# Latent attention of a hybrid diffusion backbone: outputs by token, negated maxima, three score banks, and a head's preparation spread over iterations

## What is computed

```python
def diff_attend(q1, q2, k1, k2, v, lam):
    p1 = softmax(einsum(q1, k1) * DIFF_HD ** -0.5)
    p2 = softmax(einsum(q2, k2) * DIFF_HD ** -0.5)
    return einsum(p1 - lam * p2, v)

def mla_attend(qn, qr, kn, kr, v):                 # 8 heads
    s = einsum(qn, kn) + einsum(qr, kr)            # 64 + 32 wide
    p = softmax(s * (64 + 32) ** -0.5)
    return einsum(p, v)                            # v: 64 wide
```

## Time and profile before

| | us |
|---|---|
| median of three runs | 2402.88 (2399.14 to 2410.18) |
| profiled execution | 2399.36 |
| span of its records | 2397.2 |
| TensorE busy | 2262.1 (94%) |
| VectorE, ScalarE busy | 1054.6 (44%), 855.0 (36%) |
| latent attention, layer 0 | 643.6 to 768.4 |
| latent attention, layer 1 | 1963.8 to 2040.3 |

### The profile page before, as it was taken

One profiled execution on the slowest core, in us unless ns is written; L12 is line 12 of the kernel. 1 busy time (PEld: TensorE's weight loads), 2 busy tenths in 40 slices (PEclk: granted clock), 3 DMA queues, 4 the chain that ended last, 5 costly groups with the idle time before them and its releaser, 6 DMA issues.

```text
span 2397.2 us, 29171 instructions
## 1 busy us (share of the span) xinstructions
PE 2262.1 (94%) x11992; PEld 1863.3 (78%) x11992; DVE 1054.6 (44%) x1821; ACT 855.0 (36%) x1421; POOL 78.4 (3%) x82
## 2 busy tenths in 40 slices
PE   4999999998877999999999999999999987998998
PEld 2778877786755888777787777778887875998998
DVE  3333333565455233453333344333336556456554
ACT  3322222444434222342222233222234444445443
POOL 1000000000000000000000010000010000001001
PEclk8999999999889999999999999999999999999999
DMA  7443334410110222244434334443224211454453
GB/s 296 158 173 126 141 151 147 176 71 27 51 40 27 101 92 99 70 183 158 171 110 158 138 127 174 154 149 106 94 80 173 88 60 66 154 172 150 172 198 123
DMA packets 63619, 306.09 MB, mean 128 GB/s; under 512 B 6400, under 2 KB 12288, under 8 KB 39424
## 3 DMA queue, kind: packets, MB, share of 16 engines
q1 hardware_dynamic: 54272, 237.12, 28.0%
q10 hardware_dynamic: 9216, 67.11, 7.3%
HBM read 298.97 MB, written 5.24 MB: 127 GB/s over the span
## 4 chain that ended last, share of the span: by engine, by line
PE 69%; DVE 4%; ACT 1%; issue 1%; DMA 1%; POOL 0%; DVEq 0%; ACTq 0%
PE ps L472 20%; PE ps L474 19%; PE ps L473 19%; PE ps L687 2%; PE ps L494 2%; PE ps L679 1%; DVE w_lo L1351 1%; PE ps L794 1%; PE ps L524 1%; PE ps L656 0%; PE ps L836 0%; PE ps L659 0%; PE ps L658 0%; PE ps L838 0%; DVE split_scratch L1655 0%
## 5 line engine op out<-in xcount | busy, mean ns | idle before, releaser
L1351 DVE TENSOR_TENSOR w_lo<-w_raw,w_hi 128x1024 fp32r<-128x1024 f32 (+5 forms) x516 | 513.3, 1002 | 818.0 <-ACT w_hi L929 816.7
L929 ACT CAST w_hi<-w_raw 128x1024 fp32r<-128x1024 f32 (+5 forms) x516 | 445.9, 871 | 1129.8 <-PE ps L474 1104.2
L472 PE MATMUL ps<-xn_hi,w_hi 128*128 128x512 f32 (+1 forms) x2208 | 802.3, 363 | 21.8 <-DVE xn_lo L1408 12.2
L473 PE MATMUL ps<-xn_hi,w_lo 128*128 128x512 f32 (+1 forms) x2208 | 790.6, 358 | 0.0
L474 PE MATMUL ps<-xn_lo,w_hi 128*128 128x512 f32 (+1 forms) x2208 | 790.3, 358 | 0.0
L472 PEld LDWEIGHTS ps<-xn_hi,w_hi 128*128 128x128 f32 x2208 | 421.0, 191 | 107.6 <-issue 44.8
L474 PEld LDWEIGHTS ps<-xn_lo,w_hi 128*128 128x128 f32 x2208 | 420.7, 191 | 61.4
L473 PEld LDWEIGHTS ps<-xn_hi,w_lo 128*128 128x128 f32 x2208 | 421.6, 191 | 58.1
L472 PE MATMUL ps<-split_scratch,w_hi 128*128 128x512 f32 (+1 forms) x976 | 351.8, 360 | 0.3 <-issue 0.2
L473 PE MATMUL ps<-split_scratch,w_lo 128*128 128x512 f32 (+1 forms) x976 | 349.4, 358 | 0.0
L474 PE MATMUL ps<-split_scratch,w_hi 128*128 128x512 f32 (+1 forms) x976 | 349.2, 358 | 0.0
(11 more groups left out here) (146 smaller groups left out, 1544.9 us busy)
## 6 DMA issues: line engine op xcount, KB each, us to landing
w_raw<-in_up SPq DMA_DIRECT2D x88, 1024.0 KB, 4.8
ada_w<-in_ada ACTq DMA_DIRECT2D x64, 1024.0 KB, 7.6
w_raw<-in_merge SPq DMA_DIRECT2D x48, 768.0 KB, 4.3
w_raw<-in_dn SPq DMA_DIRECT2D x32, 768.0 KB, 4.8
w_raw<-in_dn SPq DMA_DIRECT2D x32, 640.0 KB, 4.2
w_raw<-in_proj SPq DMA_DIRECT2D x20, 1024.0 KB, 4.7
w_raw<-in_wout SPq DMA_DIRECT2D x16, 512.0 KB, 3.7
scratch<-in_ada SPq DMA_DIRECT2D x6, 1024.0 KB, 7.1
```

The lines of the kernel that those rows point to most:

```text
L472: nc.tensor.matmul(out, w_hi, hi, start=first, stop=False)
L473: nc.tensor.matmul(out, w_lo, hi, start=False, stop=False)
L929: nc.scalar.copy(wh[:, u % 2, h, 0:w], raw[:, u % RAW, h, 0:w]).then_inc(hi_ready, 1)
L1351: nc.vector.tensor_tensor(wl[:, u % 2, h, 0:w], raw[:, u % RAW, h, 0:w], wh[:, u % 2, h, 0:w].bitcast(F32), ALU.subtract).then_inc(split_r ...
```

## The change

- The outputs are computed for each item, by token: the transposed weights of 128 queries are stationary, 64 columns of values move, the result is 128 tokens by 64 features, in bank 7 or 5 by turns. The weights stay unnormalized until then; VectorE multiplies the output by the reciprocal of the sum on its way to YT, which is by token. At the end of the stage TensorE turns YT back by feature, into banks 0, 1, 4, 5, and ScalarE and VectorE split from there.
- The maximum is written negated by the reduction itself. The scale is applied to the queries when ScalarE copies them (in both attentions).
- Scores use three banks (2, 3, 4) and are written two items ahead; the exponentials have three buffers, the transposed weights four.
- The preparation of a head (always banks 0 and 1, head 0 in 4 and 5) is split in steps that each stand in the iteration which HEAD_STEPS gives, after the item's own work. The product of head 0 moves into `between`, ahead of the values; the weight units are loaded in that order.

```diff
+HEAD_STEPS = dict(keys=(1, 1), queries=(2, 1), round=(3, 2), rope=(1, 1), keys_low=(2, 1), queries_low=(3, 1), split=(4, 2))
-        def mla_fill(l, t):
+        def head_at(l, t):
             per = len(item_list(l, 1)[0])
-            h, off = divmod(t + 1, per)
-            return h + 1 if t >= 0 and off == 0 and h + 1 < MLA_HEADS else None
+            for h in range(1, MLA_HEADS):
+                if t == ((h - 2) * per + per // 4 if h > 1 else -1 - per // 4):
+                    return h
+            return None
+        def step_at(l, t, step):
+            return head_at(l, t - HEAD_STEPS[step][l])
 # TensorE, between
-                piece(l, "kvv0.0")
-                piece(l, "kvv0.1")
+                mla_head(l, 0)
                 row(B_TR, 2 * nt, cols)
                 row(B_O, 3 * nt, cols)
-                piece(l, "kvv1.0")
-                piece(l, "kvv1.1")
+                for name in ("kvv0.0", "kvv0.1", "kvv1.0", "kvv1.1"):
+                    piece(l, name)
 # TensorE, mla_attention
-                    pe.wait_ge(exp_done, a0 + t - 1)
+                    if t >= 3:
+                        pe.wait_ge(exp_done, a0 + t - 2)
-                    out = ps[:, B_S + t % 2, 0:nk]
+                    out = ps[:, B_S + t % 3, 0:nk]
+                def token_outputs(t):
+                    h, _, _, _, nk = items[t]
+                    pe.wait_ge(wt_ready, a0 + t + 1)
+                    if t >= 2:
+                        pe.wait_ge(o_ready, done["pair"] + t - 1)
+                    for kc in range(nk // P):
+                        ins = nc.tensor.matmul(ps[:, B_OT[t % 2], 0:MLA_VD], WT4[:, t % 4, kc, :],
+                                               Vt[:, kc, h * MLA_VD:(h + 1) * MLA_VD],
+                                               start=(kc == 0), stop=(kc == nk // P - 1))
+                    ins.then_inc(pv_done, 1)
                 scores(0)
+                scores(1)
                 for t in range(len(items) + 3):
-                    if t + 1 < len(items):
-                        scores(t + 1)
+                    if t + 2 < len(items):
+                        scores(t + 2)
                     if 0 <= t - 2 < len(items):
-                        transposes(a0 + t - 2, items[t - 2][4], Pm[:, t % 2])
-                    if t >= 3 and items[t - 3][2] == 1:
-                        h, g, _, _, nk = items[t - 3]
-                        outputs(a0 + t - 3, g0 + g, nk, slice(64 * (h % 2), 64 * (h % 2) + 64),
-                                slice(h * MLA_VD, (h + 1) * MLA_VD))
-                    if mla_fill(l, t) is not None:
-                        mla_head(l, mla_fill(l, t))
+                        pe.wait_ge(exp_done, a0 + t - 1)
+                        transposes(a0 + t - 2, items[t - 2][4], Pm[:, (t - 2) % 3])
+                    if t >= 3:
+                        token_outputs(t - 3)
+                    if head_at(l, t) is not None:
+                        mla_head(l, head_at(l, t))
+                for c in range(4):
+                    pe.wait_ge(o_ready, done["pair"] - (3 - c) * 2 * len(item_list(l, 1)[0]))
+                    for tk in range(cols.start, cols.stop, P):
+                        ins = nc.tensor.transpose(ps[:, B_Y[c], tk:tk + P], YT[:, tk // P, c * P:(c + 1) * P], ident[:])
+                    ins.then_inc(turned_back, 1)
 # ScalarE, mla_attention
+                for t in range(-1, len(items) + 2):
+                    if 0 <= t < len(items):
+                        scores_exp(a0 + t, (B_S + t % 3,), [Pm[:, t % 3]], items[t][4], a0 + t - 2 if t >= 3 else 0)
                     if t >= 2:
-                        h, g, tq, _, nk = items[t - 2]
-                        copy_transposed(a0 + t - 2, g0 + g, tq, nk)
+                        act.wait_ge(tr_done, a0 + t - 1)
+                        if t >= 6:
+                            act.wait_ge(pv_done, done["pair"] + t - 5)
+                        nk = items[t - 2][4]
+                        nc.scalar.copy(WT4[:, (t - 2) % 4, 0:nk // P, :],
+                                       ps[:, B_TR, 0:nk].rearrange("p (k n) -> p k n", n=P)).then_inc(wt_ready, 1)
+                    if step_at(l, t, "keys") is not None:
+                        head_keys(l, step_at(l, t, "keys"))
+                    if step_at(l, t, "queries") is not None:
+                        head_queries(l, step_at(l, t, "queries"))
+                    if step_at(l, t, "round") is not None:
+                        round_unit(att(l, A_UK[step_at(l, t, "round")]) + 2)
 # VectorE
-                link(nc.vector.reduce_max(mx[:, a % 2, 0:n], src, AX_X))
-                nc.vector.tensor_scalar(nm[:, a % 2, 0:n], mx[:, a % 2, 0:n], -scale, None, ALU.mult
+                nc.vector.tensor_reduce(nm[:, a % 4, 0:n], src, axis=AX_X, op=ALU.max, negate=True
                                         ).then_inc(negmax_ready, 1)
+                for t in range(-1, len(items) + 4):
+                    if 0 <= t < len(items):
+                        negmax(a0 + t, (B_S + t % 3,), items[t][4])
                     if 1 <= t <= len(items):
-                        mla_weights(a0 + t - 1, t - 1, items[t - 1][4])
+                        dve.wait_ge(exp_done, a0 + t)
+                        b = (a0 + t - 1) % 8
+                        nc.vector.reciprocal(rr[:, b, 0:1], sm[:, b, 0:1]).then_inc(dve_chain, 1)
+                    if t >= 4:
+                        dve.wait_ge(dve_chain, inverted[t - 4])
+                        dve.wait_ge(pv_done, done["pair"] + t - 3)
+                        nc.vector.tensor_scalar(YT[:, col // P, h * MLA_VD:(h + 1) * MLA_VD],
+                                                ps[:, B_OT[t % 2], 0:MLA_VD],
+                                                rr[:, (a0 + t - 4) % 8, 0:1], None, ALU.mult).then_inc(o_ready, 1)
+                    if step_at(l, t, "rope") is not None:
+                        mla_rope(l, step_at(l, t, "rope"))
+                    if step_at(l, t, "keys_low") is not None:
+                        head_keys(l, step_at(l, t, "keys_low"))
+                    if step_at(l, t, "queries_low") is not None:
+                        head_queries(l, step_at(l, t, "queries_low"))
+                    if step_at(l, t, "split") is not None:
+                        split_unit(att(l, A_UK[step_at(l, t, "split")]) + 2)
```

More of the change, by code:

```diff
@@ L458, in _ @@
         def _(pe):
-            done = dict(norm=0, group=0, chunk=0, item=0, pair=0, head=0, four=0)
+            done = dict(norm=0, group=0, chunk=0, item=0, pair=0, head=0, four=0, weights=0)
             def half(u, h, i=0, per=0):
@@ L722, in diff_attention @@
                     if 0 <= t - 2 < len(items):
+                        pe.wait_ge(w_ready, done["weights"] + t - 1)
                         transposes(a0 + t - 2, items[t - 2][4], Pd[:, t % 2, 0])
@@ L732, in diff_attention @@
                 done["head"] += DIFF_HEADS
+                done["weights"] += len(items)
             def between(l):
@@ L808, in mla_attention @@
-                    if mla_fill(l, t) is not None:
-                        mla_head(l, mla_fill(l, t))
+                        pe.wait_ge(exp_done, a0 + t - 1)
[4 more added lines that the diff above has]
+                        mla_head(l, head_at(l, t))
                 done["item"] += len(items)
-                done["pair"] += len(pairs)
+                done["pair"] += len(items)
@@ L1054, in take_qk @@
                 bank = 4 + h % 2 if kind == "q" and h >= 2 else 2 + h if kind == "k" and h < 2 else h % 2
-                take(l, f"{kind}{'01' if h < 2 else '23'}.{h % 2}", T[kind, h][:, cols], cols, bank)
+                take(l, f"{kind}{'01' if h < 2 else '23'}.{h % 2}", T[kind, h][:, cols], cols, bank,
+                     DIFF_HD ** -0.5 if kind == "q" else 1.0)
             def take_values(l, name):
@@ L1106, in diff_attention @@
                         b = 2 + 2 * (t % 2)
-                        scores_exp(a0 + t, (b, b + 1), [Pd[:, t % 2, m] for m in range(2)], DIFF_HD ** -0.5, nk)
+                        scores_exp(a0 + t, (b, b + 1), [Pd[:, t % 2, m] for m in range(2)], nk, max(a0 + t - 1, 0))
                     if t == len(items):
@@ L1235, in _ @@
                 mla_attention(l)
-                act.wait_ge(o_ready, done["pair"])
                 for c in range(4):
-                    nc.scalar.copy(YMh[:, c, cols], YM[:, c, cols]).then_inc(ymhi_ready, 1)
+                    act.wait_ge(turned_back, 4 * l + c + 1)
+                    nc.scalar.copy(YMh[:, c, cols], ps[:, B_Y[c], cols]).then_inc(ymhi_ready, 1)
                 act.wait_ge(ydlo_ready, DIFF_HEADS * (l + 1))
@@ L1522, in low_qk, with negmax @@
                     ins.then_inc(q_ready, 1)
-            def negmax(a, banks, scale, nk):
+            def negmax(a, banks, nk):
                 dve.wait_ge(qk_done, a + 1)
@@ L1661, in mla_attention @@
                 a0, g0 = done["item"], done["pair"]
-                for h in range(2):
```

(17 more changed lines are left out.)

157 lines of the change are left out of this document (80 added, 77 removed).

## The result

The changed kernel takes 2340.48 us (median of 4 executions, 2339.46 to 2344.26), the kernel before beside it 2401.01 (2396.49 to 2410.18). The ratio is 0.9746, with a 95% interval of 0.9724 to 0.9767: some 61 us faster. The profiled execution took 2341.02 us, its span 2339.2. The forecast of 2347 was 6.5 us too high: 2.9 us by its stages (2343.9 for the profiled execution), 3.1 by the distance from profiled execution to median, which it took from the kernel before, and 0.5 because the profiled execution lies above the median here. Its parts were further off than their sum.

A forecast was written before the change was run, and what follows sets the result against it. TensorE's idle time and low clock in latent attention were taken as the loss; 42 (layer 0) + 12 (layer 1) + 1.5 (negated maxima) = 55.5 us off 2399.4 gave 2343.9, or 2347 as median; range 2335 to 2374.

The forecast's parts named there:

- layer 0's 82.6: Layer 0 latent attention: 74.9 us of work plus start, end, turning back, small waits and 1.5 ahead; before, 124.8.
- layer 1's 64.7: Layer 1 latent attention: 50.1 us of work plus waits, turning back, margin and 0.9 ahead; before, 76.5.
- (a): Layer 0 latent attention: exponentials come late and ScalarE's order becomes the bound; 2372 us, chance 0.22.
- (e): Whole change: the loop is bound by something unseen and nothing moves; 2403 us, chance 0.02.
- hand drawing: Layer 0 latent attention: one head's schedule laid out for each engine, TensorE the bound, 10.2 us a head.
- whole iteration: Layer 0: the third bank puts a whole iteration between maximum and use, said against late exponentials.
- 0.105 per instruction: Outputs by token: us for each 64-column product, so an item costs 0.84 or 0.42 us.
- Rival (b): Outputs by token: the load of 128 columns is not covered, 0.19 us a product; 2374 us, chance 0.05.
- 1.4 us for seven waits in differential attention: Negated maxima, layer 0: seven waits, 8.5 us in all, shortened by 0.2 us each.
- third piece of the values: Ahead of layer 0's latent stage: it waits for head 0's bank to be copied; 1.5 us, between 0 and 3.
- Rival (c): Layer 1: the 1.4 us wait isn't there, as ScalarE reaches the keys before the copy is due; 2338 us, chance 0.11.
- rival (d): Both latent stages: the clock stays low with more transposes and small products, 106 us added; 2453 us, chance 0.05.

The follow-up runs named there:

- all three pairs: 64 against 128 moving columns: changed kernel (2340.48, 2336.78 us); with layer 1's keys and queries before the copy (2335.94, 2332.50); with ends moved too (2329.69, 2324.62).
- one kernel with 64 columns: Changed kernel with layer 1's keys and queries before the copy, head 1's steps earlier, last rounding and split later, output products of 64 columns: 2329.69 us.
- the one with the order alone: Changed kernel, with ScalarE in layer 1 taking the next head's keys and queries ahead of the copy of transposed weights: 2335.94 us, ratio 0.9728.

## Why the prediction was right in sum

By stage, profiled execution against profiled execution (2343.9 predicted, 2341.0 measured):

| | predicted | measured |
|---|---|---|
| ahead of the stage of layer 0, against before | +0.1 | -1.4 |
| latent attention, layer 0 | 81.1 | 75.4 |
| between the stages | 1196.2 | 1190.9 |
| latent attention, layer 1 | 63.8 | 73.6 |
| the rest | 359.1 | 358.8 |

(1.5 of layer 0's 82.6 and 0.9 of layer 1's 64.7 were put ahead of the stages.) A miss of +9.8 in layer 1 was hidden by two of -5.7 and -5.3, the latter within what unedited code varies by. That the sum came so close is luck in part.

**Layer 0: the mechanism held, the work was priced too high.** TensorE is the bound, with a steady head period, clock 1.00 and 1.5 us of waits on exponentials: rivals (a) and (e) are out. The preparation is 3.52, as priced. The period is 9.55 and not 10.2, because transposes cost 0.44 and 0.22, not 0.53 and 0.31; outputs 0.81 and 0.37, not 0.84 and 0.42; scores 0.70 to 0.78, not 0.80. The prices of the earlier trace rows held the change-over to the next kind of product, which was another one then. That and the turning back make 76.7 predicted against 72.65 measured; idle time was 2.8, not 4.4. What the prediction did not see is which part carries it: its hand drawing contains the spread but gives it no price. Undone, it costs 32 us. The "whole iteration" that it credits to the third bank moves the scores, not the iteration at which the exponential is due, and the stage differs by 1.9 us, nearly all of it one fall of the clock.

**Outputs by token.** 0.105 per instruction was taken from two-column products; it is 0.81 / 8 = 0.101. Rival (b) is out. Products twice as wide cost nothing either: layer 0 took 75.60 us with 128 columns. The Trainium skill (TensorE: Matmul & The Clock Gate, Back-to-back issue gap) says that the spacing is set by load and product together; that the width is free beside a load of 128 columns agrees with it.

**Negated maxima.** The mis-sized term: 1.4 us for seven waits in differential attention. The chain is shorter by the 0.21 us that was read off, the exponential of the earlier trace rows at 506.23 now starts at 506.02:

```profile
504.77 2.35 DVE L1567 TENSOR_REDUCE score_negmax<-ps 128x2 f32<-128x1024 f32 x2
506.02 0.69 ACT L1064 ACTIVATE scratch<-ps,score_negmax 128x512 f32<-128x512 f32 x1 [1.89 <-DVE score_negmax L1567]
```

But the waits fell from 8.5 to 8.3 in all and the stage by 0.2. Seven waits named after one engine are not seven places where its last link counts. Ahead of the latent stage 1.5 us were charged for the third piece of the values; it waited 0.6, and the stretch became 1.2 shorter instead (67.9 for 69.1).

**Layer 1: waits right, clock wrong.** The wait for the queries' low part was drawn at 1.4 and is 1.36 in four heads of six, 1.07 and 1.61 in the others; the one at the start was drawn at 2.6 and is 2.54. Rival (c) is out. Idle time sums to 13.2; the 2.6 at the start, 8.0 for the heads, 0.3 at the end and 1.6 of margin are 12.5. One wait was missed, 2.6 us in front of the transposes near the end: the merge unit's rounding and split stand ahead of the last maxima; moved away, the wait went. The heads, said to be 8.3 apart, are 8.1 at the high clock (1946.19 - 1938.10) and 9.6 to 11.3 where it falls. Nearly the whole miss is in the busy time: 50.1 and 1.2 predicted, 60.4 measured, 9.1 of the 9.8 us. The step that failed is the case against rival (d), "a steady window of layer 1, with transposes and 1.5 us of idle time, is at 1.00", carried over to a stage in which the 256-column products it held had become 64-column ones. In the kernel before, waits of 1.44 to 1.57 us in steady heads were not followed by a fall (1980 to 2022, clock 1.00); the prediction drew new waits of the same length and gave them no price in clock, and with 64-column products three of them had one. With 128 columns and idle time down from 13.2 to 4.3 us the stage ran at 1.00 and was busy for 50.05, the priced work to 1.3 us.

**Rival (d)** had a part in layer 1: clock 0.84, 9 us of the 106 that it reckoned; layer 0 was at 1.00. The page's mechanism beside it (TensorE: Matmul & The Clock Gate, A second HAM failure mode: psum-queue depth-cycling, in the Trainium skill) is short idle times that come from going on to another bank. That falls stand behind short idle times agrees with it: here behind waits of 1.3 to 2.6 us in layer 1. That the banks make them is not shown: TensorE waits there for low parts and for copies, and two banks in place of three leave the clock where it was (layer 0 at 0.98 and 1.00, layer 1 at 0.86 and 0.84). No run here does without cycling.

**Layer 1 with two banks.** The kernel with two banks had its stage of layer 1 at 63.0 us, 10.6 less than the changed one, with 6.2 us idle: one item ahead, a head's first scores are due an iteration later and its queries' low part is in time. That the look-ahead, not a bank, makes the wait is confirmed by three banks and one ahead: the four waits on low parts in front of score products (4.3 us together) are gone. The stretch between the stages, 1196.1 in that kernel, hid most of the gain from its median.

## What to carry to other kernels

Where engines work off their queues in order, look for the longest lump between two links of the cycle that feeds the bound engine, and cut it before you buy a buffer: spreading was worth 32 us here with the rest in place, the third bank 1.9 at most. A further item of look-ahead also makes the next head's operands due an item sooner, so where a head has only two items it can cost more than it gives. Price every block at the change-over it will have after the change, and do not carry a window's granted clock to another mix of products: a wait of 1.4 us that cost only itself beside 256-column products was followed by the low level beside 64-column ones.

## What the runs showed of the hardware

The granted clock fell to 0.50 behind a wait of 2.61 us and stayed there for 10.8 us with TensorE never idle, in transposes and fp32 products of 64 moving columns. With 128 moving columns the stage of layer 1 was at a higher clock in all three pairs (0.84 to 0.95, 0.83 to 0.97, 0.94 to 1.00), at no cost for each product, since 128 and 64 columns both came every 0.10 us or so. But layer 0 with 64 columns was at 1.00, and so were the last 9 us of layer 1 in one kernel with 64 columns:

```profile
1963.00:1972.10 9.10, 9.10 (x79) 8.81 (x78) 3.76 (x13) 6.47 (x15) 0.00 (x0) 1.00 0.00 1
```

The same instructions can run at either level. In that last kernel the wait of 2.6 us in front of them had been moved away; in the changed kernel and in the one with the order alone, where they ran at 0.50, it stood there. In every latent stage that was looked at in half-us windows, the low level came only during a wait or within 2 us of one, but not behind each, and the shortest waits with a fall behind them were 0.90 and 0.59 us, one after the other (two banks, layer 0). What picks the waits that are followed by it is not settled here. The width makes the low level rarer in the profiles; the medians of the three pairs differ by 3.7, 3.4 and 5.1 us, each within the uncertainty of its pair.
